# A one-core decoder step: reordering SP's loads and three DVE steps in the attention pairs

## What is computed

```python
q, gate = jnp.split(rms_norm(x, norm_g) @ w_in, 2, axis=-1)
q = rms_norm(q.reshape(bsz, t, B_HEADS, B_DH), q_norm)      # k, v: one shared projection
s = jnp.einsum('bqhd,bkhd->bhqk', qi, k_all) * scale
logits = jnp.where(mask, s + (c_q[..., :, None] - c_t[..., None, :]), -jnp.inf)
p = jax.nn.softmax(logits, axis=-1)                          # c: running sum of log forget gates
o = jnp.einsum('bhqk,bkhd->bqhd', p, v_all)
return x + (o * silu(gate)) @ w_o
```

## Time and profile before

| | |
|---|---|
| runs | 1549.47, 1555.58, 1561.13 us (median 1555.58) |
| the profiled execution | 1561.13 us, span 1559.4 us, mean granted clock 0.989 |
| busy share of the span | PE 96%, DVE 65%, ACT 44%, POOL 27% |
| busy PE in the pairs | 86.60 of 92 us from 860 to 952, 88.87 of 92 us from 1044 to 1136 |
| the chain that ended last | PE 72%, DMA 12%, DVE 7%, ACT 3%, SPq 3% |
| moved by DMA | 296.81 MB, a mean of 190 GB/s |

### The profile page before, as it was taken

The page is one execution under the profiler, slowest core; times in us unless marked ns, Lnnn a source line. Parts: engine busy times, 40 slices in busy tenths (PEclk is TensorE's granted clock), DMA queues, the critical chain, the costliest instruction groups (busy, mean ns, idle before and its releaser), DMA issues.

```text
span 1559.4 us, 23169 instructions
## 1 busy us (share of the span) xinstructions
PE 1499.6 (96%) x8353; PEld 1097.7 (70%) x8353; DVE 1009.4 (65%) x1987; ACT 684.1 (44%) x1380; POOL 419.6 (27%) x335
## 2 busy tenths in 40 slices
PE   7999999999999999999999989989998999998998
PEld 6888888888888865447776767667676766764443
DVE  5869687877868673226486866768586675856421
ACT  4445554454555542222464554535455454545100
POOL 5022212121231001012243434144344414432200
PEclk9999999999999999999999999999999999999999
DMA  9682937658292743323346785775767577589641
GB/s 272 175 253 81 278 104 209 173 153 237 77 297 98 226 166 99 89 62 100 109 143 194 250 264 175 252 248 197 231 230 249 185 241 249 208 278 337 223 145 56
DMA packets 289411, 296.81 MB, mean 190 GB/s; under 512 B 25722, under 2 KB 247098, under 8 KB 289298
## 3 DMA queue, kind: packets, MB, share of 16 engines
q1 hardware_dynamic: 278162, 258.75, 53.3%
q0 software_dynamic: 11136, 36.59, 6.6%
HBM read 239.90 MB, written 122.50 MB: 232 GB/s over the span
## 4 chain that ended last, share of the span: by engine, by line
PE 72%; DMA 12%; DVE 7%; ACT 3%; SPq 3%; issue 2%; POOL 0%; DVEq 0%; ACTq 0%; POOLq 0%
PE psum L2109 34%; PE psum L2133 7%; PE psum L2616 7%; DMA block_rows<-arena 6%; DMA arena<-block_rows 4%; PE psum L2442 4%; PE psum L2186 3%; PE psum L2416 3%; PE psum L2072 2%; PE psum L2474 2%; SPq L669 2%; DVE arena L1793 1%; DVE arena L474 1%; PE psum L2376 1%; DMA arena<-in_w_o_b 1%
## 5 line engine op out<-in xcount | busy, mean ns | idle before, releaser
L2109 PE MATMUL psum<-arena 128*128 128x252 f32 (+1 forms) x3472 | 812.8, 384 | 2.2 <-DVE arena L1429 2.2
L2109 PEld LDWEIGHTS psum<-arena 128*128 128x128 f32 x3472 | 642.4, 190 | 120.7 <-issue 25.6
L937 POOL TENSOR_TENSOR arena<-arena 128x1024 f32<-128x1024 f32 x64 | 152.1, 2377 | 360.4 <-DMA arena<-k_pages 355.7
L1429 DVE TENSOR_TENSOR arena<-arena,psum 128x252 f32<-128x252 f32 (+1 forms) x310 | 129.8, 419 | 175.7 <-PE psum L2109 158.5
L2616 PE MATMUL psum<-arena 128*128 128x512 f32 x256 | 115.9, 604 | 3.7 <-DMA arena<-in_w_o_b 2.1
L1012 ACT COPY arena<-psum 128x252 f32<-128x252 f32 (+1 forms) x124 | 46.3, 373 | 160.5 <-PE psum L2109 160.5
L2133 PE MATMUL psum<-arena 128*128 128x512 f32 x256 | 113.0, 594 | 0.1
L2442 PE MATMUL psum<-arena 128*64 128x256 f32 (+1 forms) x640 | 81.2, 405 | 21.7 <-DMA arena<-block_rows 21.7
L2616 PEld LDWEIGHTS psum<-arena 128*128 128x128 f32 x256 | 47.5, 192 | 61.7 <-issue 56.0
L2442 PEld LDWEIGHTS psum<-arena 128*64 128x64 f32 x640 | 47.8, 151 | 59.4 <-DMA arena<-block_rows 24.6
L2133 PEld LDWEIGHTS psum<-arena 128*128 128x128 f32 x256 | 47.5, 190 | 57.4 <-issue 56.5
(11 more groups left out here) (267 smaller groups left out, 2151.0 us busy)
## 6 DMA issues: line engine op xcount, KB each, us to landing
k_pages<-in_cache_k SPq DMA_DIRECT2D x64, 512.0 KB, 6.6
v_pages<-in_cache_v SPq DMA_DIRECT2D x64, 512.0 KB, 7.2
arena<-k_pages SPq DMA_DIRECT2D x64, 512.0 KB, 7.0
arena<-v_pages SPq DMA_DIRECT2D x64, 512.0 KB, 6.8
arena<-in_w_in_a SPq DMA_DIRECT2D x32, 512.0 KB, 6.8
arena<-in_x_prompt SPq DMA_DIRECT2D x16, 512.0 KB, 7.6
arena<-in_w_kv SPq DMA_DIRECT2D x16, 512.0 KB, 6.2
arena<-in_w_in_b SPq DMA_DIRECT2D x16, 512.0 KB, 7.9
```

Of the source, the lines that this page charges most:

```text
L937: pool.tensor_tensor(k_ring[:, m % 2], k_ring[:, m % 2], q_all[:, m % S:m % S + 1, :].broadcast_to([P, PAGES, P]), ALU.mult).then_inc(kq_m ...
L1429: dve.tensor_tensor(out, more, bank[n % 2][:, 0:size(u)], ALU.add).then_inc(of.by_dve, 1)
L2109: ins = pe.matmul(bank[n % 2][:, 0:size(u)], w[:, k, :], x[:, k, :], start=(k == 0 and r in (0, 1, 3, 4)), stop=(k == HK - 1), skip_group_ ...
```

## The change

Nothing is computed otherwise, and the instructions are the same; only their order and three waits of SP change.

- SP, pairs 0 to 6: `k_in(m + 6)` is no longer issued between `store_row(p, 7)` and `load_row(p, 7)`, but at the head of the next pair (there it is `k_in(m - 2)`). `hi_in` of the next pair moves from that pair's middle to right behind `load_row(p, 7)`, and `lo_in(p + 1)` from the middle of the pair to its head. `v_in(p - 1, 1)` and `k_in(m)` move ahead of the loads of `w_v` and `w_g`.
- SP, last pair: the same for `k_in(m - 2)`; `v_in` and `k_in(m)` change places and `hi_in` is already done; the residual rows 0 and 1 move from ahead of `store_row(p, 4)` to behind `k_in(m + 4)`.
- DVE: `gate_in(p)` moves behind `shift(p - 1, 1)`, and `score(m + 1)` ahead of `turn_blocks(p, 4)`. `norm(p + 1, 0)` moves from ahead of `row_max(p, 7)` to behind `top_of(p, 0)`. `norm(p + 1, 1)` moves from behind `row_max(p, 7)` to between the two halves of `turn_blocks(p, 7)`.

```diff
--- before.py
+++ after.py
@@ -630,8 +630,6 @@
                 sp.dma_start(c_lo[p % 2], c_dram[0, 2 * p:2 * p + 2].rearrange("x n -> (x n)").partition_broadcast(P)).then_inc(lo_loaded[p % 2], 16)
 
             def hi_in(p):
-                if p:
-                    sp.wait_ge(max_done, 2 * TT * p)
                 sp.dma_start(c_hi, c_dram[1, 2 * p:2 * p + 2].rearrange("x n -> (x n)").partition_broadcast(P)).then_inc(hi_loaded, 16)
 
             sp.wait_ge(y_done, 2 * (TT + 1))
@@ -682,22 +680,22 @@
             def pair(p):
                 m = S * p
                 if p:
-                    k_in(m - 1)
+                    sp.wait_ge(max_done, 2 * TT * p)
+                lo_in(p + 1)
+                if p:
+                    k_in(m - 2, m - 1)
+                    v_in(p - 1, 1)
+                    k_in(m)
                 sp.wait_ge(b_units.done, vg_b(p, 14))
                 load_wb(sp, w_v, w_kv_d, p + 1, 1, w_v_loaded)
                 load_wb(sp, w_g, w_qg_d, p + 1, 1, w_g_loaded)
                 if p:
-                    k_in(m)
-                    v_in(p - 1, 1)
-                    hi_in(p)
                     k_in(m + 1)
                 k_in(m + 2, m + 3)
                 store_row(p, 4)
                 load_row(p, 4)
                 if p:
                     v_in(p, 0)
-                    sp.wait_ge(max_done, 2 * TT * p)
-                lo_in(p + 1)
                 k_in(m + 4)
                 store_row(p, 5)
                 load_row(p, 5)
@@ -713,21 +711,20 @@
                 store_row(p, 6)
                 load_row(p, 6)
                 store_row(p, 7)
-                k_in(m + 6)
                 load_row(p, 7)
+                sp.wait_ge(max_done, 2 * TT * (p + 1))
+                hi_in(p + 1)
 
             def last():
 
                 p, m = PAIRS - 1, S * (PAIRS - 1)
-                k_in(m - 1)
-                sp.wait_ge(max_done, 2 * TT * p)
                 w_ob_in(early_b, 2)
                 sp.wait_ge(s_done, scored(p - 1, TT - 1, 1))
                 for h in range(2):
                     sp.dma_start(o_y[h], o_dram[h]).then_inc(early_b, 16)
+                k_in(m - 2, m - 1)
+                v_in(p - 1, 1)
                 k_in(m)
-                v_in(p - 1, 1)
-                hi_in(p)
                 sp.wait_ge(b_units.done, vg_b(p, 14))
                 sp.wait_ge(ob_stored, 16 * OWN)
                 for h in range(3, OWN):
@@ -738,12 +735,12 @@
                 k_in(m + 2)
                 w_ob_in(w_ob_loaded, AH - 2, AH - 1)
                 k_in(m + 3)
-                resb_in(0)
-                resb_in(1)
                 store_row(p, 4)
                 load_row(p, 4)
                 v_in(p, 0)
                 k_in(m + 4)
+                resb_in(0)
+                resb_in(1)
                 store_row(p, 5)
                 load_row(p, 5)
                 k_in(m + 5)
@@ -1967,13 +1964,13 @@
                 turn_v(p, 3)
                 kq(5)
                 row_max(p, 4)
-                gate_in(p)
                 fin(p, 1)
                 kq(6)
                 if p:
                     shift(p - 1, 1)
+                gate_in(p)
+                score(m + 1)
                 turn_blocks(p, 4, 0, 1)
-                score(m + 1)
                 kq(8)
                 row_max(p, 5)
                 if p:
@@ -2000,20 +1997,20 @@
                 turn_blocks(p, 6, 0, 1)
                 vg(3)
                 vg(4)
-                if nxt:
-                    norm(p + 1, 0)
                 row_max(p, 7)
-                if nxt:
-                    norm(p + 1, 1)
                 vg(5)
                 fin(p, 2)
                 if nxt:
                     top_of(p, 0)
+                    norm(p + 1, 0)
                 vg(6)
                 last(3)
                 if nxt:
                     shift(p, 0)
-                turn_blocks(p, 7, 0, 1)
+                turn_blocks(p, 7, 0)
+                if nxt:
+                    norm(p + 1, 1)
+                turn_blocks(p, 7, 1)
                 if not nxt:
                     top_of(p, 0)
                 vg(8)
```

## The result

The changed kernel takes 1576.51 us (median of 4 runs, 1570.41 to 1579.2) against 1557.69 for the kernel before beside it: a ratio of 1.0124, with a 95% interval of 1.0089 to 1.0158. It is slower by 19 us, outside the range that was forecast. Its profiled execution took 1576.44 us, with a span of 1574.7 (before: 1559.4) and a mean granted clock of 0.991.

A forecast was written before the change was run, and what follows sets the result against it. PE, busy 96% of the span, was taken as the bound; -9.1 (load) + 4.9 (norms) - 1.65 (clock) + 4.3 (weights) - 2.9 (last pair) = -4.4 us, 1551.2 us against the median of 1555.58; range 1539 to 1567.

The forecast's parts named there:

- What bounds the kernel: PE is busy 96% of the span, so only what PE waits for can be won or lost.
- Row 7's load: Without the page ahead, `load_row(p, 7)` lands earlier, gaining 1.3 us in each of seven pairs: -9.1 us.
- The clock: Behind `weighted(p, 3)`, one of six stalls, pair 5's, falls under 1.26 us and avoids slow clock: -1.65 us, bounds 0 to -9.9.
- The weights: Behind values and page, `w_v` lands 1.6 to 3.6 us too late for DVE: +4.3 us, bounds -2.9 to +16.
- the collision: POOL's `times_q(m)` beside DVE's `scale_w` makes that take 3.03 us instead of 1.22; pairs 2, 3 and 5 already collide.
- very late: Rival: `w_v` over about 12.5 us behind `decode`; six pairs lose 3.2 us plus 1.65 clock, +26, 1573 us; chance 0.12.
- The norms: Around `turn_blocks(p, 7)`: `norm(p + 1, 0)` costs nothing, `norm(p + 1, 1)` 3.9 us in three pairs, 1 in four: +4.9.
- What would show it: Signs in the profile, for the weights: DVE's `scale_w` waiting for `in_w_kv`, PE over 2.4 us for ACT in `turn_rows`.
- Pages and small steps: Later `k_in(m + 6)`, and `gate_in` and `score(m + 1)` ahead of `turn_blocks(p, 4)`: nothing, at worst +0.5 in eight pairs.
- The last pair: Output weights land earlier, -3.9 us with clock; `y_add(0)` comes about 1 us later; net -2.9, bounds -3.9 and 0.

The follow-up runs named there:

- four values alone: Kernel before with only the loads around row 7 changed, plus the four value loads ahead of `w_v` and `k_in(m)` behind the weights: ratio 0.9961.
- values and page: Kernel after with both norms back at their old places around `row_max(p, 7)`, values and page still ahead of `w_v`: 1556.33 us, ratio 0.9998 to the kernel before.
- combined version: Kernel after with `w_v`, `w_g`, `k_in(m)`, values in this order, and both norms and the residual rows at their old places: 1536.27 us, ratio 0.9888.
- weights first, then the page: Kernel after with `w_v`, `w_g`, then `k_in(m)`, then the four value loads, the order of the kernel before: 1548.17 us, ratio 0.9949.
- one norm between the halves: Kernel before with only the loads around row 7 changed, plus `norm(p + 1, 1)` between the halves of `turn_blocks(p, 7)`: 1548.48 us, ratio 0.9955.

## Why the prediction was wrong

- *What bounds the kernel.* Right: PE's waits decide, and their changes add up to the span's within 2.5 us (17.8 against 15.3).
- *Row 7's load.* Right in kind, too small. It lands 5.3 to 6.3 us behind its issue instead of 5.2 to 8.7, and `weighted(p, 3)` lost 12.8 us of waits where this part stands alone (21.7 to 8.9). I had 9.1. Together with the clock this part is worth 17 us.
- *The clock.* The step that failed here is "falls under 1.26 us": a stall need not be that short. Behind stalls of 1.49 to 1.92 us the kernel after runs `weighted` in 3.53 us. I counted one slow stretch of six as won; all six are gone, and one is new in pair 0 (848.15, 5.18 us), so 8.25 us at 1.65. But five others came back behind `turn_rows(p, 3)`, some 1.5 us each: the transposes 1.96 instead of 1.27 us, the unit behind them 2.71 instead of the 1.87 that it takes at full clock. The clock gained nothing on the whole (0.989 before, 0.991 after).
- *The weights.* The term that decided. Mis-sized was one number in it: `w_v` was to land 11.3 to 13.3 us behind `decode`, and landed 14.2 behind in pair 2, 13.9 to 14.6 in all six. I took 9.5 to 11.5 us for the values and the DMA behind them from the earlier trace rows, 12.4 was measured (951.04 + 9.8 - 948.43), and 1.8 more for `w_v`, which was right. One term in it stood at nothing: the wait of `k_in(m)` for `score(m - 2)`, behind which SP issues `w_v` 2.3 to 5.2 us after `decode` instead of 2.0. The four values alone gave 11.2 us (median), and values and page 14.3; of these 3.1 us more the page's bytes explain 1.2 to 1.8, and no run separates the rest. The rest of the step held: DVE wanted it 9.8 us behind `decode`, the collision added 0.5, and 4.43 + 0.53 of lateness came out as 3.97 us of PE's, so 1.0 of slack where I had 0.9. So the mechanism was that of the rival "very late", including its price. Six waits of 21.0 us less the 2.4 of before, and 1.5 of slow clock in five pairs, make 26 us, and the rival had +26. Its condition, `w_v` later than about 12.5 us behind `decode`, I had before me with 11.3 to 13.3 as bounds, and gave it 0.12. That chance was the error more than the number: a price that jumps inside the bounds of its own input calls for an even share on both sides.
- *The norms.* The second failed step. Row 0's scores wait 4.5 us longer, close to the 4.9 forecast, which is luck, and DVE's waits for row 6's store did shrink, to 1.06 and 1.14 us in two pairs. But in this order of SP's loads the scores would have waited 1.1 us only, so the norms cost 7.9 there. `norm(p + 1, 0)` was costed at nothing because a wait of DVE hid it; POOL's product made it 2 to 3 us long in four of the six pairs. For `norm(p + 1, 1)` I let the shrinking wait for row 6's store pay in pairs 1, 2, 4 and 5, where it was 0.50, 2.71, 0.95 and 3.56 us. With row 7's load alone changed and both norms at their old places it is 0, 0.44, 0 and 0.42: it shrinks without the norm, so it hides nothing of it. The norm costs its 1.25 us in all seven pairs, 8.7 us, and 9.6 were measured; I had 3.9 in three pairs and 1 in the other four. In all they cost 9.5 to 9.6 us with the weights in time (9.6 for one of the two alone), and 20 with the weights late, against my 4.9. The difference between these two is hardly larger than their intervals, and in the profiled executions it is smaller: 16.5 us of span with the weights late (1574.7 and 1558.2), 13.8 with them in time (1547.6 and 1533.8). Its cause stays open. What `norm(p + 1, 0)` costs by itself does too.
- *What would show it.* Each sign named for the weights appeared: DVE's wait for `in_w_kv` in all six pairs, and far more than 2.4 us for ACT. So did the 1.25 us between the halves and the end of the stalls for `in_w_o_b`.
- *Pages and small steps.* Nothing in pairs 1 to 6, as forecast. In the last pair the late page cost 2.3 us of PE.
- *The last pair.* The stalls for output weights went, -2.1 as forecast. The page above, and 2.2 us more of waiting for `y_add(0)` (1 was forecast, from the residual rows), took more than that back. Behind that wait two causes overlap, a small addition beside POOL's product and the residual rows.

By the ratios the runs lead from the kernel before to the kernel after in two ways: -17 for row 7's load (combined version), then +17 for the weights and +20 for the norms, or +10 for the norms first and +27 for the weights; both end at +19. (For the weights, alone on the kernel before: +22.) The forecast's own sum had -10.75 for load and clock, +4.3 for the weights, +4.9 for the norms and -2.9 for the last pair.

## What to carry to other kernels

When a DMA is moved ahead of another, price what it delays by the bytes ahead of it in the queue against the time at which the late one is wanted; if the bounds of the landing span that time, the two outcomes are near equal rivals and the steep one is no edge case. If the moved DMA waits for something in the issuing engine's list, that wait delays everything behind it as well, beyond its bytes. When a step is moved into a wait of its engine, look which other engine works beside it there, and follow everything that is queued behind it, the store as well as the next matmul.

## What the runs showed of the hardware

- An operation with both inputs in SBUF (`arena` in the rows) is long on DVE beside POOL's product of a page when POOL was first. `norm` takes 3.24 us instead of 1.28 and the 64 x 4 addition 2.33 instead of 0.16. In both, the end is that of POOL's instruction plus the rest of DVE's own: 1199.86 + 2.34 = 1202.20, then 1.10 to 1203.30. The Trainium skill ("SBUF — State Buffer", SBUF: two separate sides) says that the pair of ports which the two engines share is a lock and not a split, held for the whole instruction of the one that came first. The trace agrees: a tiny instruction waits for the rest of POOL's as a large one does. An addition that reads PSUM is not held up: `y_add(0)` at 1427.45 takes its usual 1.29 us for two, beside POOL's product from 1426.30 to 1428.64 (weights first, then the page).
- SP's issuing instruction itself is longer when much is under way. The load of `w_g`, issued behind values, page and `w_v` in pair 2 of the kernel after, took 5.27 us to issue, against 0.3 to 0.6 us for those ahead of it; in the other five pairs it took 5.45, 5.32, 3.39, 4.96 and 0.91, and 0.58 to 0.60 in all six of the kernel before, where only `w_v` stands right ahead of it. Whatever stands behind it is issued that much later.
- The length of a stall does not settle alone whether the clock falls behind it. `weighted(p, 3)` took 5.18 us at a mean granted clock of 0.67, part of it at 1.2 GHz, behind 1.97 and 2.10 us of stall, and 3.53 at 1.00 (2.4 GHz) behind 2.17, in one and the same run (one norm between the halves).
